# Loading the FFN gate and up weights in the stage before the FFN, and opening the planner's cost constants to configuration

## The reference

```
u      = rms_norm(h, g_mix)
proj   = u @ w_in + b_in                     # attention 768, RWKV 1824, gates 2048 columns
y_attn = sliding_window_sink_attention(rope(q), rope(k), v)      # window 128, 8 heads of 64
y_rwkv = rwkv7_time_mix(...)                 # 8 heads, recurrent state 64x64
merged = sigmoid(gate_a) * (y_attn @ w_ba) + sigmoid(gate_r) * (y_rwkv @ w_br)
h      = h + merged @ w_o
f      = rms_norm(h, g_ffn)
h      = h + (silu(f @ w_fg) * (f @ w_fu)) @ w_fd      # hidden width 2816
out    = rms_norm(h, g_final)                # meta positions dropped
```

## Time and profile before

| | us |
|---|---|
| median of 2 runs | 4742.86 (4742.12 to 4743.6) |
| the profiled execution | 4560.85 |
| its span, slowest core (4) | 4559.4 |
| spans of the eight cores | 4546.8 to 4559.4 |
| stage A1, first instruction to the barrier | 0 to about 2771 |
| stage A2 | about 2771 to 3334 |
| stage B | about 3334 to 4559 |

### The profile page before, as it was taken

How to read it: one execution, slowest core, us unless ns; L and a number is a source line. 1 busy time by engine, 2 the same in 40 slices (tenths; PEclk the granted TensorE clock), 3 DMA queues, 4 the chain that set the end, 5 groups by cost and what they waited for, 6 DMA issues and landing times.

```text
span 4559.4 us, 113126 instructions; the slowest of 8 cores (4546.8 to 4559.4 us)
## 1 busy us (share of the span) xinstructions
PE 3434.4 (75%) x45780; PEld 2751.0 (60%) x45937; DVE 1969.4 (43%) x3635; ACT 1596.0 (35%) x3790; POOL 1085.0 (24%) x964
## 2 busy tenths in 40 slices
PE   3767767677666776777767764888846999999998
PEld 2555555555555555555555554777735777777776
DVE  1455465564655546556455551222212333333333
ACT  1334334343343433434333332555511222222222
POOL 2323223232332322323223231111110001001001
PEclk7666566676666656667566656999968999999999
DMA  5000000000000000000000004122185111111110
GB/s 90 7 8 10 14 10 14 8 10 14 10 14 8 10 14 10 14 8 10 14 9 10 12 5 93 65 69 71 60 131 95 36 36 47 37 36 36 48 37 27
DMA packets 70642, 143.48 MB, mean 31 GB/s; under 512 B 5616, under 2 KB 35568, under 8 KB 70000
## 3 DMA queue, kind: packets, MB, share of 16 engines
q1 hardware_dynamic: 43344, 104.77, 6.9%
q0 software_dynamic: 26784, 31.46, 4.8%
HBM read 134.12 MB, written 33.55 MB: 37 GB/s over the span
## 4 chain that ended last, share of the span: by engine, by line
PE 53%; POOL 13%; DVE 12%; ACT 9%; issue 8%; DMA 3%; another core or an unknown queue 1%; DVEq 0%; ACTq 0%; POOLq 0%; SPq 0%
PE psc L902 12%; PE psc L917 7%; PE ps L469 5%; POOL a_pf L480 3%; PE psb L796 3%; POOL a_pf L478 3%; POOL a_pf L477 3%; PE psc L883 2%; DVE a_B L587 2%; PE ps L557 2%; ACT a_sg L800 2%; PE ps L572 2%; PE ps L573 2%; POOL a_t L824 2%; PE ps L312 1%
## 5 line engine op out<-in xcount | busy, mean ns | idle before, releaser
L796 PE MATMUL psb<-a_uT,a_wgate 128*128 128x128 bf16 x4096 | 288.4, 239 | 102.3 <-ACT a_sg L800 88.7
L902 PE MATMUL psc<-b_fT,b_wu 128*128 128x128 bf16 x5632 | 353.0, 221 | 13.3 <-DMA b_wu<-w_fu 13.3
L902 PE MATMUL psc<-b_fT,b_wg 128*128 128x128 bf16 x5632 | 351.1, 221 | 9.8 <-DMA b_wg<-w_fg 9.8
L902 PEld LDWEIGHTS psc<-b_fT,b_wg 128*128 128x128 bf16 x5632 | 334.0, 99 | 33.6 <-issue 11.0
L902 PEld LDWEIGHTS psc<-b_fT,b_wu 128*128 128x128 bf16 x5632 | 330.4, 99 | 21.6 <-issue 14.2
L796 PEld LDWEIGHTS psb<-a_uT,a_wgate 128*128 128x128 bf16 x4096 | 276.6, 109 | 108.6 <-issue 108.0
L917 PE MATMUL psc<-b_wd,b_aT 128*128 128x512 bf16 x1345 | 303.1, 381 | 32.1 <-DMA b_wd<-w_fd 27.9
L469 PE MATMUL ps<-a_uT,a_wfm 128*128 128x128 bf16 x4224 | 305.2, 240 | 29.0 <-DVE a_stg L472 18.4
L469 PEld LDWEIGHTS ps<-a_uT,a_wfm 128*128 128x128 bf16 x4224 | 283.0, 109 | 46.2 <-issue 37.0
L460 PE MATMUL ps<-a_wqkv,a_uT 128*128 128x256 bf16 x264 | 61.6, 414 | 325.6 <-DVE a_qkv L459 325.6
L460 PEld LDWEIGHTS ps<-a_wqkv,a_uT 128*128 128x128 bf16 x264 | 34.3, 139 | 353.3 <-issue 340.9
(11 more groups left out here) (245 smaller groups left out, 7718.5 us busy)
## 6 DMA issues: line engine op xcount, KB each, us to landing
a_xb<-xe SPq DMA_DIRECT2D x65, 512.0 KB, 3.7
b_xb<-xe SPq DMA_DIRECT2D x32, 512.0 KB, 4.4
out<-b_xsB SPq DMA_DIRECT2D x32, 512.0 KB, 2.9
a_yT<-yscr SPq DMA_DIRECT2D x32, 256.0 KB, 3.9
mscr<-a_mT SPq DMA_DIRECT2D x32, 256.0 KB, 2.2
b_mT<-mscr SPq DMA_DIRECT2D x32, 256.0 KB, 4.5
b_wd<-w_fd POOLq DMA_DIRECT2D x2, 2816.0 KB, 114.2
b_wg<-w_fg POOLq DMA_DIRECT2D x5, 1024.0 KB, 58.2
```

The lines of the kernel that those rows point to most:

```text
L796: fns.append(lambda e, i=i, col=col, kc=kc, bank=bank: e.matmul(bank[:, i * 128:(i + 1) * 128], wgate[:, kc, col:col + 128], uT[:, kc, :], ...
L902: fns.append(lambda e, i=i, fc=fc, kc=kc, bank=bank, wt=wt: e.matmul(bank[:, i * 128:(i + 1) * 128], wt[:, kc, fc * 128:(fc + 1) * 128], f ...
```

## The change

The buffers of `wg` and `wu` are taken between stages A1 and A2 and kept to the end, and their 12 loads are issued in stage A2, right behind the 6 loads of that stage. Stage B then issues only the loads of `wo` and of the two halves of `wd`. The planner's constants (hop, cost of an instruction, a random spread of the costs, a bonus to each stream) can be read from environment variables.

```diff
-        HOP = 0.3
+        import os as _os0
+        import random as _random
+        _cfg = _os0.environ.get("KCFG", "0,0.3,0.1,0.03,0.5,0.0").split(",")
+        _rng = _random.Random(int(_cfg[0]))
+        HOP = float(_cfg[1]); KPE = float(_cfg[2]); KPS = float(_cfg[3]); KVD = float(_cfg[4]); JIT = float(_cfg[5])
...
+            if JIT > 0:
+                dur = dur * (1.0 + JIT * (_rng.random() - 0.5))
...
-        def V(fn, R=(), W=(), d=0.5):
+        def V(fn, R=(), W=(), d=None):
+            d = KVD if d is None else d
...
-                d = n_ * (0.03 if ST["small"] else 0.1) + 0.1
+                d = n_ * (KPS if ST["small"] else KPE) + 0.1
...
-        def run(gens):
+        def run(gens, bonus=None):
...
+            if bonus is None:
+                bonus = [0.0] * len(gens)
...
-                        t = est_start(h)
+                        t = est_start(h) - bonus[i]
...
+                B_SEQ, B_PRE, B_ATT, B_HEAD = [float(v) for v in _os.environ.get("KB", "0,0,0,0").split(",")]
...
-                    run(par(streams, wts))
+                    run(streams, bon)
                 S.barrier()
+
+        es_bw = ExitStack()
+        pre_w = {}
+        if "B" in phases:
+            sbw_ = mk_alloc(es_bw, "bw_")
+            pre_w["wg"] = sbw_("wg", [128, 8, DFF], BF16)
+            pre_w["wu"] = sbw_("wu", [128, 8, DFF], BF16)
+
+        def load_bw():
+            wg, wu = pre_w["wg"], pre_w["wu"]
...
+            for g in range(ngrp_):
+                c0, c1 = 512 * g, min(512 * (g + 1), DFF)
+                wg_b.append(wload_blk(wg, wg[:, :, c0:c1], w_fg.rearrange("(c p) n -> p c n", p=128)[:, :, c0:c1]))
+                wu_b.append(wload_blk(wu, wu[:, :, c0:c1], w_fu.rearrange("(c p) n -> p c n", p=128)[:, :, c0:c1]))
...
                 S.finalize(ch_w, [cst, pfm])
+                if "B" in phases:
+                    load_bw()
...
-                wg = sb("wg", [128, 8, DFF], BF16)
-                wu = sb("wu", [128, 8, DFF], BF16)
+                wg, wu = pre_w["wg"], pre_w["wu"]
                 wd = sb("wd", [128, NFC, D], BF16)
                 wo_b = wload_blk(wo, wo[:], w_o.rearrange("(c p) n -> p c n", p=128))
...
-                for g in range(ngrp_):
-                    c0, c1 = 512 * g, min(512 * (g + 1), DFF)
...
+                if "wg_b" not in pre_w:
+                    load_bw()
+                wg_b, wu_b = pre_w["wg_b"], pre_w["wu_b"]
```

More of the change, by code:

```diff
@@ L239, in mkop, with A @@
             return None
-        def V(fn, R=(), W=(), d=0.5):
+        def V(fn, R=(), W=(), d=None):
+            d = KVD if d is None else d
             return mkop("dve", fn, R, W, d)
-        def A(fn, R=(), W=(), d=0.5):
+        def A(fn, R=(), W=(), d=None):
+            d = KVD if d is None else d
             return mkop("act", fn, R, W, d)
@@ L738, in build_program @@
                 _skip = _os.environ.get("KSKIP", "")
+                B_SEQ, B_PRE, B_ATT, B_HEAD = [float(v) for v in _os.environ.get("KB", "0,0,0,0").split(",")]
                 for i in range(nt):
                     streams = [seq(i)] if "seq" not in _skip else []
-                    wts = [W_SEQ] if "seq" not in _skip else []
+                    bon = [B_SEQ] if "seq" not in _skip else []
                     if i + 1 < nt:
@@ L744, in build_program @@
                             streams += [pre(i + 1)]
-                            wts += [W_PRE]
+                            bon += [B_PRE]
                         if "att" not in _skip:
                             streams += [attention(i + 1)]
-                            wts += [W_ATT]
+                            bon += [B_ATT]
                     if i + 2 < nt:
                         streams.append(head(i + 2))
-                        wts.append(W_HEAD)
-                    run(par(streams, wts))
+                        bon.append(B_HEAD)
+                    run(streams, bon)
                 S.barrier()
+        es_bw = ExitStack()
[6 more added lines that the diff above has]
+            wg, wu = pre_w["wg"], pre_w["wu"]
+            ngrp_ = (NFC + 3) // 4
+            wg_b = []
+            wu_b = []
+            for g in range(ngrp_):
+                c0, c1 = 512 * g, min(512 * (g + 1), DFF)
+                wg_b.append(wload_blk(wg, wg[:, :, c0:c1], w_fg.rearrange("(c p) n -> p c n", p=128)[:, :, c0:c1]))
+                wu_b.append(wload_blk(wu, wu[:, :, c0:c1], w_fu.rearrange("(c p) n -> p c n", p=128)[:, :, c0:c1]))
+            pre_w["wg_b"] = wg_b
+            pre_w["wu_b"] = wu_b
         if "A2" in phases:
@@ L850, in build_program @@
                 wo = sb("wo", [128, 8, D], BF16)
-                wg = sb("wg", [128, 8, DFF], BF16)
-                wu = sb("wu", [128, 8, DFF], BF16)
+                wg, wu = pre_w["wg"], pre_w["wu"]
                 wd = sb("wd", [128, NFC, D], BF16)
                 wo_b = wload_blk(wo, wo[:], w_o.rearrange("(c p) n -> p c n", p=128))
-                ngrp_ = (NFC + 3) // 4
-                wg_b = []
-                wu_b = []
-                for g in range(ngrp_):
-                    c0, c1 = 512 * g, min(512 * (g + 1), DFF)
-                    wg_b.append(wload_blk(wg, wg[:, :, c0:c1], w_fg.rearrange("(c p) n -> p c n", p=128)[:, :, c0:c1]))
-                    wu_b.append(wload_blk(wu, wu[:, :, c0:c1], w_fu.rearrange("(c p) n -> p c n", p=128)[:, :, c0:c1]))
+                if "wg_b" not in pre_w:
+                    load_bw()
+                wg_b, wu_b = pre_w["wg_b"], pre_w["wu_b"]
                 wd_b = [wload_blk(wd, wd[:, 11 * hh:11 * hh + 11, :], w_fd.rearrange("(c p) n -> p c n", p=128)[:, 11 * hh:11 * hh + 11, :]) for hh in range(2)]
@@ L943, in build_program @@
             S.barrier()
+        es_bw.close()
     return nc
```

## The result

The changed kernel takes 0.9883 of the time of the one before (95% interval 0.9859 to 0.9908), 1.2% less: within the 2% that count as no change, though the interval excludes 1. The forecast, 4688 against 4742.86, is 0.9884. Some executions of each kernel are longer by up to four per cent, with a lower granted clock on some cores; the ratios leave out all but the mildest of these, and the times given for a kernel are of the others (4558 to 4565 us before, 4502 to 4504 after, where two mild ones at 4520 and 4522 count in the ratio). The profiled executions took 4560.85 and 4503.73 us, a ratio of 0.9875, 57.1 us apart where 55 were forecast.

The account below looks back on a forecast made before the run. At B's start PE waits for weight loads; behind that PE is the bound. B's gain of 67 us less 12 us for `xb` in A2 gives -55 us: 4742.86 to 4688 us, range 4668 to 4722.

Parts of the forecast that it names:

- The planner: Planner code: with no variable set, each compute engine gets the same instructions in the same order; cost nothing.
- B up to `wd`: Stage B's start: 36.8 us go before PE asks for `wd`, and the whole 27.9 us wait for `wd` too.
- The margin: Stage B's start: both halves of `wd` are in 11 us before PE asks for them.
- The cold start behind the standstill: Stage B: first 21 matmuls with `wd` take 4.70 us instead of 7.21 if PE no longer stops; 2.5 us go.
- The issues on GpSimd: A2's start: twelve more issues delay the power step 6.6 us, covered by PE's later waits; cost nothing.
- The waits on `xb`: A2's run: `xb` lands in 10.2 us beside the new loads, costing 2.5 us a tile, 12 us over five.
- Rival 1: A2: each `xb` load needs 15 to 19 us beside the stream, costing 37 to 58 us; chance 0.18.
- the prediction's own step: A2's `xb`: small queue gets half the engine at worst, so store and load take about 11.8 us from the store's issue.
- Rival 2: A2: the 18 loads share the engines instead of landing in issue order, `wbr` lands late, time 4760; chance 0.03.
- Rivals 3 and 4: First: B wins 15 to 25 us less, chance 0.10. Second: timed runs move for a reason outside the terms, chance 0.05.

Follow-up runs that it names:

- e1: Changed kernel with the 12 loads of `wg` and `wu` issued in stage B again, early buffers and planner code kept; profiled at 4559.2 us.
- e7: Changed kernel with only groups 0 to 2 of `wg` and `wu` loaded in A2, groups 3 to 5 in B behind `wo`; ratio to before 0.9909.
- e3: Changed kernel with the 12 loads issued behind the first two power steps on GpSimd instead of ahead; ratio to before 0.9873.
- e2: Changed kernel with A2's `xb` loads issued one tile earlier, into three buffers; ratio to before 0.9854.
- e5: Changed kernel with `wo` also loaded in A2, behind the last `wu` block; ratio to before 0.9858.
- e4: Changed kernel with the 12 loads of `wg` and `wu` issued ahead of A2's own 6 loads; ratio to before 0.9997.
- e6: Changed kernel with the edits of e2, e3 and e5 together; ratio to before 0.9817.
- e8: e6 with B's first SyncE loads reordered, `mT` ahead of `xb` and `gfin` behind the first tile's loads; median 4476.7 us, ratio to before 0.9796.

## Why the prediction was right

The mechanism was right: B's start lost its waits, and the price was `xb`. Term by term the sum was -67 for B and +12 for A2; the means of the eight cores give -70.2 and +11.7 (and +0.5 in A1). That the second comes so close is in part luck, as is said below. The forecast was taken off 4742.86; taken off the profiled 4560.85 its ratio would have been 0.9879 in place of 0.9884, so nothing hung on that choice. The prediction also held 2% to be what a measurement of this kernel can tell; the interval came out at a quarter of a per cent to either side.

**The planner: nothing.** Right; the orders are the same and e1 has the old times.

**B up to `wd`, -36.8 and -27.9.** Right. PE's list from the first `wg` matmul took 25.46 us against 25.2, which is 64.4 us less than the 89.9 of the earlier trace rows where 64.7 were forecast; in the mean of the cores the start of the stage up to `wd` is 67.4 us shorter. The margin was mis-sized: the sum took `wd`'s halves at 32.3 us behind `wo`, and they took some 38 (3372.1 to 3409.9), so 5 us were left of the 11. Why they move more slowly there no run shows. It decided nothing here; e7 shows what it costs when the margin is gone: with half of the blocks put ahead of `wd` again, PE waits 27.2 us for it in the mean.

**The cold start behind the standstill (the first matmuls with `wd` at 7.21 us in place of 4.70), -2.5.** Measured -2.8, and +2.5 again in e7.

**The issues on GpSimd: nothing, being covered.** The answer was right and the size wrong. The step said 6.6 us of delay; it was 15.3 on the power step and 12 to 13 at PE, because GpSimd was held at its 17th and 18th load, 7.8 us in all. e3 took the delay away and won 0.4 us. The cover had less to spare than was thought: PE still waited 1.0 us for the last gate block.

**The waits on `xb`, +12.** The term was right in kind and nearly in size: landings of 10.0 for 10.2 taken, 11.2 us in 4 waits on the slowest core for 12 in 5, 9.0 in the mean. e2 removes it by lead alone, e7 halves it with half the stream. Rival 1, with landings of 15 to 19, is excluded for A2: behind the stage's first tiles no `xb` load of the changed kernel took longer than 10.7 us on any core. Such landings do occur at B's start, behind other loads of the same queue (14.9 for `mT` in e5), which was the ground given against it. The Trainium skill ("DMA: Bandwidth & Descriptors", Queues, rings and completion order) lets an engine alternate between its queues packet by packet. That a queue gets half of the engine by this is the prediction's own step, which the section does not state. It gave 11.8 us from the store's issue to the landing of `xb`, and the rows have 10.4 (2834.35 to 2844.8), so they agree with it roughly.

**Left out of the sum:** 1.0 us for 12 more channels at A2's barrier, and about 1.3 us by which A2's first merge is late, in e3 too, where GpSimd is on time. The second is hardly more than the spread between kernels with the same loads (55.6 before, 56.2 in e1). I put it down to the new blocks already moving while `wba` and `wbr` land; no run isolates it. These two and waits of 9.0 us make up most of the 11.7 that A2 grew, which the sum had put on `xb` alone.

**Rival 2, loads that share.** Excluded: GpSimd's loads of a stage land in the order of their issue on every core of every run, and e4 shows what it costs to stand behind others, 66 us of A2 (636.3 against 570.4). **Rivals 3 and 4** did not occur.

## What to carry to other kernels

A prefetch is worth the waits that it removes up to the next thing asked for, not the bytes that it moves: the same 12 loads moved to the same stage won 58 us behind its own loads and nothing ahead of them (e4), and with half of them moved PE waited 27 us for the last load in line, `wd` (e7). Put it behind the loads that the current stage waits for. Then look for what is loaded beside it with too little lead (here `xb` had 7 to 8.5 us, and its landing went from 3.7 to 10), and give that one a tile more. When the first wait of a stage is gone, the next is found in the order of the small loads of another queue.

## What the runs showed of the hardware

GpSimd's issue of loads was held though its own instructions take 0.87 us. In the changed kernel the 17th load began at 2789.83, 0.3 us after the first one landed (2773.75 + 15.8), and the 18th at 2796.34, 0.3 us after the second. It is not a count of 16 loads: in e4, where the loads with 1024 rows come first, the 16th was held, until 2790.35, and so was the 18th, of 512 rows. Counted in rows of the source (1024 for a block of `wgate`, `wg` or `wu`, 512 for `wba` or `wbr`), each held load would have brought the rows in flight to 16,384, and the loads held in e2, e5, e6 and e8 are such too. The kernel before had 16,128 rows (16,368 packets on that queue in the trace) in flight at B's start and was not held. Nor is it a count of bytes, since these 15 loads came to 18.5 MB on chip, and the 16 in flight in the changed kernel to 16. So a long burst of such loads seems to stop the issuing engine between these two figures, and what stands behind them on it waits for a landing. The count is read from kernels made for other questions; none was made to vary it.
